# Two query heads per score bank for the first query tile, one bank for the meta scores, and another order of the opening loads

## The reference

```python
h = rms_norm(x, norm_g)
proj = einsum('btd,de->bte', h, w_in)    # q, k, v, gate_a, u_b, gate_b, q_idx, k_idx, w_idx, merge
# 8 heads of 64; one k, one v, one k_idx; rope on q, k, q_idx, k_idx
s = einsum('bqhd,bkd->bqhk', qib, k_idx)                  # the indexer's scores
score = einsum('bqhk,bqh->bqk', relu(s), wib * scale)     # masked by chunk of 64
_, sel = top_k(score, 64)
p = softmax(einsum('bqhd,bqkd->bqhk', qb, k[sel]) * 64 ** -0.5)
attn = einsum('bqhk,bqkd->bqhd', p, v[sel])               # then w_a; a pooling branch, w_b, w_out
```

## Time and profile before

| | |
|---|---|
| median of three runs | 1218.49 us (1218.14 to 1219.87) |
| the profiled execution | 1218.49 us |
| its span, first to last instruction | 1216.7 us |
| PE busy | 1205.7 us (99%), 8521 matmul records |
| PEld busy | 1117.4 us (92%) |
| ACT busy | 726.7 us (60%) |
| DVE busy | 638.6 us (52%) |
| POOL busy | 978.8 us (80%) |
| SP's queue | 207.74 MB, 51.4% of the 16 DMA engines' span |

### The profile page before, as it was taken

How to read it: one execution, slowest core, us unless ns; L and a number is a source line. 1 busy time by engine, 2 the same in 40 slices (tenths; PEclk the granted TensorE clock), 3 DMA queues, 4 the chain that set the end, 5 groups by cost and what they waited for, 6 DMA issues and landing times.

```text
span 1216.7 us, 22059 instructions
## 1 busy us (share of the span) xinstructions
PE 1205.7 (99%) x8521; PEld 1117.4 (92%) x8521; DVE 638.6 (52%) x1463; ACT 726.7 (60%) x1355; POOL 978.8 (80%) x772
## 2 busy tenths in 40 slices
PE   9999999999999999999999999999999999999998
PEld 8999999999998888889999999998889988888886
DVE  6585555765645444312946789853556235444411
ACT  6556756566757666545645677774357347666642
POOL 4775678876679999898889767789899749998795
PEclk9999999999999999999999999999999999999999
DMA  7543445544446555555466645555466435655553
GB/s 254 165 156 122 157 139 184 163 159 137 144 156 199 194 189 188 179 192 189 157 208 211 193 160 176 181 169 190 166 205 226 161 112 178 206 186 183 188 190 104
DMA packets 60056, 213.37 MB, mean 175 GB/s; under 512 B 6672, under 2 KB 6960, under 8 KB 59824
## 3 DMA queue, kind: packets, MB, share of 16 engines
q1 hardware_dynamic: 57600, 207.74, 51.4%
q10 hardware_dynamic: 2352, 4.23, 1.3%
HBM read 210.86 MB, written 1.08 MB: 174 GB/s over the span
## 4 chain that ended last, share of the span: by engine, by line
PE 91%; DVE 6%; ACT 2%; issue 0%; DMA 0%; SPq 0%; DVEq 0%
PE bank L395 23%; PE bank L366 14%; PE bank L368 14%; PE bank L367 14%; PE bank L398 12%; PE bank L1590 2%; PE bank L1592 2%; PE bank L1591 2%; DVE ar L1970 1%; PE bank L1029 1%; PE bank L940 1%; DVE ar L2082 1%; PE bank L2400 1%; PE bank L2402 1%; PE bank L2401 1%; PE bank L2452 1%
## 5 line engine op out<-in xcount | busy, mean ns | idle before, releaser
L325 POOL TENSOR_TENSOR wlo<-raw,whi 128x512 fp32r<-128x512 f32 x768 | 978.6, 1306 | 225.1 <-ACT whi L317 223.8
L317 ACT ACTIVATE whi<-raw 128x1024 fp32r<-128x1024 f32 x387 | 405.0, 1053 | 59.1 <-DMA raw<-w_dram 28.1
L366 PE MATMUL bank<-xx,whi 128*128 128x256 f32 (+1 forms) x1216 | 352.0, 290 | 0.0
L368 PE MATMUL bank<-xx,wlo 128*128 128x256 f32 (+1 forms) x1216 | 343.5, 283 | 0.0
L367 PE MATMUL bank<-xx,whi 128*128 128x256 f32 (+1 forms) x1216 | 343.4, 282 | 0.0
L366 PEld LDWEIGHTS bank<-xx,whi 128*128 128x128 f32 x1216 | 228.8, 188 | 2.8 <-issue 1.2
L367 PEld LDWEIGHTS bank<-xx,whi 128*128 128x128 f32 x1216 | 229.2, 189 | 1.3 <-issue 1.0
L368 PEld LDWEIGHTS bank<-xx,wlo 128*128 128x128 f32 x1216 | 228.6, 188 | 0.0
L395 PE MATMUL bank<-xx,whi 128*128 128x512 f32 x768 | 193.3, 393 | 0.0
L395 PEld LDWEIGHTS bank<-xx,whi 128*128 128x128 f32 x768 | 137.5, 188 | 24.7
L366 PE MATMUL bank<-yy,whi 128*128 128x256 f32 (+1 forms) x390 | 113.3, 291 | 0.0
(11 more groups left out here) (316 smaller groups left out, 1603.8 us busy)
## 6 DMA issues: line engine op xcount, KB each, us to landing
raw<-w_dram SPq DMA_DIRECT2D x387, 512.0 KB, 3.3
ar<-sums_dram ACTq DMA_DIRECT2D x16, 256.0 KB, 4.0
h<-x_dram SPq DMA_DIRECT2D x4, 272.0 KB, 5.9
ar<-mem_dram SPq DMA_DIRECT2D x1, 1024.0 KB, 7.1
out_dram<-ar SPq DMA_DIRECT2D x4, 256.0 KB, 2.2
cst<-con_dram SPq DMA_DIRECT2D x1, 789.0 KB, 7.5
ar<-fin_dram SPq DMA_DIRECT2D x1, 512.0 KB, 5.4
cst<-con_dram SPq DMA_DIRECT2D x1, 134.0 KB, 6.8
```

The source lines that it names most:

```text
L317: e.activation(whi[:, i % NSPL, :], raw[:, i % NRAW, :], ACT.Copy).then_inc(*whi_done.done(i))
L325: return e.tensor_tensor(wlo[:, q, c0:c1], raw[:, i % NRAW, c0:c1], whi[:, q, c0:c1].bitcast(F), ALU.subtract)
L366: e.matmul(o, wh, both[:, 0, :], start=(i == 0), stop=False)
L368: m = e.matmul(o, wl, both[:, 0, :], start=False, stop=(i == len(feed) - 1))
```

## The change

`WARM` goes from 12 to 10. SP loads slot 0 in two halves with the parameters in between, and all pieces of `h` are issued from ACT's queue, at the start of ACT's stream, as five DMAs (chunk 0, chunk 1, then pairs). ACT splits the two halves of slot 0 by themselves; the squares and DVE's additions come behind all high and low parts. `norm_sums` moves from behind the sixth tile of qi 0 to behind the third of qi 1, and `norm_spread` from behind the third tile of qi 1 to behind its eighth and last. ACT splits slot 4 ahead of the norm's root. For query tile 0, in both layers, two heads share a bank, for the indexer's scores (one relu over both) and for the attention's scores (DVE waits for the second of the two); the meta scores lie in one bank.

```diff
--- before.py
+++ after.py
@@ -19,7 +19,7 @@
 TILES = 8
 SLOT = TILES * 128
 NRAW = 4
-WARM = 12
+WARM = 10
 NSPL = 5
 LOOK = 3
 YCOLS = 24 * 256 + 32
@@ -303,6 +303,18 @@
                 e.wait_ge(*low_event(i - NRAW, half))
         e.dma_start(raw[:, i % NRAW, :], None if wts is None else wts[i]).then_inc(sems[f"w{i % NRAW}"], 16)
 
+    def load_half(e, half):
+
+        at = slice(SLOT // 2 * half, SLOT // 2 * (half + 1))
+        e.dma_start(raw[:, 0, at], None if wts is None else wts[0][:, at]).then_inc(sems["w0" if half else "l_w"], 16)
+
+    def split_half(e, half):
+
+        at = slice(SLOT // 2 * half, SLOT // 2 * (half + 1))
+        e.wait_ge(sems["w0" if half else "l_w"], 16)
+        e.activation(whi[:, 0, at], raw[:, 0, at], ACT.Copy).then_inc(*(whi_done.done(0) if half else whi_done.done(0, 0)))
+        split["n"] = half
+
     split = {"n": 0}
 
     def split_high(e, upto):
@@ -337,7 +349,7 @@
 
         slot, j = divmod(len(plan), TILES)
         plan.append(desc)
-        e.wait_ge(*whi_done.of(slot))
+        e.wait_ge(*(whi_done.of(slot) if slot or j >= TILES // 2 else whi_done.of(0, 0)))
         if low:
             low_tile(e, slot, j)
         q = slot % NSPL
@@ -625,30 +637,30 @@
 
     def half_low(e, i, half):
 
-        e.wait_ge(*whi_done.of(i))
+        e.wait_ge(*(whi_done.of(i) if i or half else whi_done.of(0, 0)))
         split_low(e, i, SLOT // 2 * half, SLOT // 2 * (half + 1)).then_inc(*wlo_half.done(i, half))
 
     def prologue_scalar(e):
 
         N, x = norms["n0"], tens["sq"][:, 0, 0:2]
+        for c, n in ((0, 1), (1, 1), (2, 2), (4, 2), (6, 2)):
+            e.dma_start(h[:, c:c + n, :], small[:, c:c + n, :]).then_inc(sems[H_LOADS[c]], 16)
         e.wait_ge(*v_step.of("one"))
         e.activation(x[:, 1:2], x[:, 0:1], ACT.Sqrt).then_inc(*s_step.done("table", "n0"))
-        split_high(e, 1)
+        split_half(e, 0)
         e.wait_ge(sems["l_p"], 16)
         for c in range(8):
             e.wait_ge(sems[H_LOADS[c]], 16)
             norm_high(e, N, c)
-            if c == 1:
-                e.wait_ge(*s_step.of("table", "n0"))
-                norm_square(e, N, 0)
-                norm_square(e, N, 1)
+            if c == 0:
+                split_half(e, 1)
             if c == 3:
-                norm_square(e, N, 2)
                 split_high(e, 2)
         split_high(e, 3)
-        for c in range(3, 8):
+        e.wait_ge(*s_step.of("table", "n0"))
+        for c in range(8):
             norm_square(e, N, c)
-            if c == 4:
+            if c == 2:
                 split_high(e, 4)
         e.wait_ge(sems["l_c1"], 16)
 
@@ -661,10 +673,8 @@
         norm_low(e, N, 0)
         norm_low(e, N, 1)
         half_low(e, 0, 1)
-        norm_add(e, N, 1)
         norm_low(e, N, 2)
         norm_low(e, N, 3)
-        norm_add(e, N, 2)
         half_low(e, 1, 0)
         norm_low(e, N, 4)
         norm_low(e, N, 5)
@@ -672,12 +682,11 @@
         norm_low(e, N, 6)
         norm_low(e, N, 7)
         half_low(e, 2, 0)
-        norm_add(e, N, 3)
-        norm_add(e, N, 4)
+        norm_add(e, N, 1)
+        norm_add(e, N, 2)
         half_low(e, 3, 0)
-        norm_add(e, N, 5)
-        norm_add(e, N, 6)
-        norm_add(e, N, 7)
+        for c in range(3, 8):
+            norm_add(e, N, c)
         e.wait_ge(sems["l_c1"], 16)
 
     def prologue_tensor(e):
@@ -929,12 +938,27 @@
 
     PER_TICK = 2
 
+    def take_scores(e, K, kind, t, hh):
+
+        l = K.l
+        if t:
+            side_.take(e, kind, l, t, hh)
+            side_.give((kind, l, t, hh), (v_step, (kind, l, t, hh)))
+        elif hh % 2 == 0:
+            side_.take(e, kind, l, t, hh // 2)
+            side_.give((kind, l, t, hh // 2), (v_step, (kind, l, t, hh + 1)))
+        return scores_of(K, kind, t, hh)
+
+    def scores_of(K, kind, t, hh):
+
+        nk = K.keys(t)[1]
+        return side_.at(kind, K.l, t, hh)[:, 0:nk] if t else side_.at(kind, K.l, t, hh // 2)[:, nk * (hh % 2):][:, 0:nk]
+
     def indexer_tensor(e, K, t):
         l = K.l
         c0, nk, _ = K.keys(t)
         for hh in range(8):
-            o = side_.take(e, "ix", l, t, hh)[:, 0:nk]
-            side_.give(("ix", l, t, hh), (v_step, ("ix", l, t, hh)))
+            o = take_scores(e, K, "ix", t, hh)
             e.wait_ge(*s_step.of("ki2", l))
             e.wait_ge(*v_step.of("rope", l, "qi", 3))
             e.matmul(o, K.qisc[:, hh, c0:c0 + 128], K.kiT[:, 0:nk], start=True, stop=True).then_inc(
@@ -948,9 +972,13 @@
         l = K.l
         c0, nk, _ = K.keys(t)
         for hh in range(8):
-            o = side_.at("ix", l, t, hh)[:, 0:nk]
             e.wait_ge(*piece.of("ix", l, t, hh))
-            e.activation(o, o, ACT.Relu).then_inc(*s_out.done("ix", l, t, hh))
+            if t:
+                o = scores_of(K, "ix", t, hh)
+                e.activation(o, o, ACT.Relu).then_inc(*s_out.done("ix", l, t, hh))
+            elif hh % 2:
+                o = side_.at("ix", l, t, hh // 2)[:, 0:2 * nk]
+                e.activation(o, o, ACT.Relu).then_inc(*s_out.done("ix", l, t, hh))
             if hh % PER_TICK == PER_TICK - 1:
                 yield
         for _ in range(8 // PER_TICK):
@@ -964,9 +992,9 @@
         for h0 in range(0, 8, PER_TICK):
             yield
             for hh in range(h0, h0 + PER_TICK):
-                e.wait_ge(*s_out.of("ix", l, t, hh))
+                e.wait_ge(*s_out.of("ix", l, t, hh if t else hh | 1))
                 e.wait_ge(*v_step.of("ix", l, t, hh - 1) if hh else v_step.of("w", l))
-                e.scalar_tensor_tensor(ac, side_.at("ix", l, t, hh)[:, 0:nk], K.V[:, t, 64 + hh:65 + hh],
+                e.scalar_tensor_tensor(ac, scores_of(K, "ix", t, hh), K.V[:, t, 64 + hh:65 + hh],
                                        ac if hh else vis, ALU.mult, ALU.add).then_inc(*v_step.done("ix", l, t, hh))
             yield
         for r in range(8):
@@ -1022,8 +1050,7 @@
                 e.wait_ge(*s_step.of("lm", l, t, 7))
                 e.transpose(o[:, 0:128], K.LM, ident).then_inc(*piece.done("pm", l, t))
             for hh in (2 * s, 2 * s + 1) if s < 4 else ():
-                o = side_.take(e, "qk", l, t, hh)[:, 0:nk]
-                side_.give(("qk", l, t, hh), (v_step, ("qk", l, t, hh)))
+                o = take_scores(e, K, "qk", t, hh)
                 e.wait_ge(*v_step.of("rope", l, "q", 3))
                 e.wait_ge(*s_step.of("k2", l))
                 e.matmul(o, K.qcs[:, hh, c0:c0 + 128], K.kT[:, 0:nk], start=True, stop=True).then_inc(
@@ -1082,13 +1109,13 @@
                 e.reciprocal(K.rs[:, hs], K.sm[:, hs]).then_inc(*v_step.done("rs", l, t, s - 2))
             yield
             for hh in (2 * s, 2 * s + 1) if s < 4 else ():
-                e.wait_ge(*piece.of("qk", l, t, hh))
+                e.wait_ge(*piece.of("qk", l, t, hh if t else hh | 1))
                 e.wait_ge(*v_step.of("sel", l, t))
                 if t:
                     e.wait_ge(*s_out.of("pt", l, 0, hh // 2))
                     e.wait_ge(*s_step.of("lm", l, 0, hh))
                 e.wait_ge(*v_step.of("qrec", l))
-                e.scalar_tensor_tensor(K.L[:, hh, 0:nk], side_.at("qk", l, t, hh)[:, 0:nk], K.rq[:, t, hh:hh + 1], bs,
+                e.scalar_tensor_tensor(K.L[:, hh, 0:nk], scores_of(K, "qk", t, hh), K.rq[:, t, hh:hh + 1], bs,
                                        ALU.mult, ALU.add).then_inc(*v_step.done("qk", l, t, hh))
             yield
         ob = side_.at("ob", l, t)
@@ -1114,13 +1141,14 @@
 
     def meta_tensor(e, K):
         l = K.l
-        pair = [side_.take(e, "mqk", l, half) for half in range(2)]
+        o = side_.take(e, "mqk", l)
+        side_.give(("mqk", l), (v_step, ("mqk", l, 1)))
         e.wait_ge(*v_step.of("rope", l, "q", 3))
         e.wait_ge(*s_step.of("k2", l))
         for half in range(2):
-            side_.give(("mqk", l, half), (v_step, ("mqk", l, half)))
             for j in range(4):
-                m = e.matmul(pair[half][0:16, 16 * j:16 * j + 16], K.qcs[:, 2 * j + half, 0:16], K.kT[:, 0:16],
+                at = 64 * half + 16 * j
+                m = e.matmul(o[0:16, at:at + 16], K.qcs[:, 2 * j + half, 0:16], K.kT[:, 0:16],
                              start=True, stop=True)
             m.then_inc(*piece.done("mqk", l, half))
         yield
@@ -1173,9 +1201,9 @@
         rq = K.rq[0:META, 2, :].rearrange("p (j i) -> p i j", i=2)
         e.wait_ge(*v_step.of("mrq", l))
         for half in range(2):
-            e.wait_ge(*piece.of("mqk", l, half))
+            e.wait_ge(*piece.of("mqk", l, 1))
             e.tensor_tensor(Lm[:, 4 * half:4 * half + 4, :],
-                            side_.at("mqk", l, half)[0:META, 0:64].rearrange("p (h k) -> p h k", k=16),
+                            side_.at("mqk", l)[0:META, 64 * half:64 * half + 64].rearrange("p (h k) -> p h k", k=16),
                             rq[:, half, :].unsqueeze(2).broadcast_to([META, 4, 16]), ALU.mult).then_inc(
```

(15 more changed lines are left out.)

## The result

The changed kernel takes 1221.54 us (median of 22 executions, 1218.45 to 1222.51); the kernel before, timed beside it, 1219.02 (22 executions, 1218.08 to 1220.26). The ratio is 1.0017, with a 95% interval of 1.0011 to 1.0023: slower by 0.17%, some 2 us (the medians lie 2.5 us apart). The kernel before spreads over 2.2 us, the changed one over 4.1, in two groups. Seven executions took 1218.45 to 1219.88 (median 1219.16), all at a mean granted clock of TensorE of 0.999. Fifteen took 1220.15 to 1222.51, twelve of them at 0.996 or 0.997 and three at 0.998, which executions of the kernel before show too.

What follows compares the result with a forecast made beforehand. PE, busy 99% of the span, was taken as the bound, so its shifts were added: -0.1 (Part 2) +1.5 (Part 3) -0.8 (Part 4) = +0.6 on 1218.49, giving 1219.1 us; range 1216.8 to 1221.4.

Steps and rivals of the forecast that it cites:

- (a): Rival, opening: two queues land slot 1 by 7.3 us, qi 0 starts 1.7 earlier; 1217.5 us, low end 1217.0; chance 0.18.
- Part 1: Opening: ACT is free at 4.4 us and PE's first matmul starts at 6.2, 1.4 us earlier.
- Part 2: Run up to qi 0: slot 1 lands at 8.8 us, qi 0 starts at 14.1; shift -0.1 us.
- Part 3: Norm's row: a new 1.9 us wait ahead of the keys' squares' sums, the sums' 0.3 wait gone; +1.5 us.
- Part 4: Banks: waits of 0.5 us at the meta scores and 0.4 in layer 1 go; -0.8 us taken.
- (c): Rival, opening turns: TensorE's clock rises later, 48 matmuls each about 0.1 us longer; +3.0 on the sum, 1222.1; chance 0.08.

Runs made afterwards that it cites:

- f1_cover: Changed kernel with 14 warm-up matmuls, four fillers ahead of chunk 1 and eight between the spread and L745; 1218.92 us against 1218.66 for the kernel before.
- e2_opening: Changed kernel without its bank part, so the opening alone; 1222.53 us against 1218.94 for the kernel before.
- e4_sp: Changed kernel with the pieces of h issued from SP's queue again; 1220.77 us against 1218.94 for the kernel before.
- f2_norm_back: Changed kernel with the norm's squares, additions, sums and spread placed as in the kernel before; 1218.29 us against 1218.66 for the kernel before.
- f3_norm_late: Kernel before with the bank part and the later norm, loads and 12 warm-up matmuls as before; 1219.53 us against 1218.66 for the kernel before.
- e1_banks: Kernel before with the bank part of the change alone, opening as before; 1217.18 us against 1218.94 for the kernel before.
- f4_warm10: Kernel before with the bank part and 10 warm-up matmuls in place of 12; 1217.44 us against 1218.66 for the kernel before.
- e3_fill: Changed kernel with 14 warm-up matmuls and four fillers ahead of chunk 1; 1220.39 us against 1218.94 for the kernel before.

## Why the prediction was right and where it was wrong

**The sum at full clock was near, the direction was luck.** The forecast was +0.6. The changed kernel's seven executions at 0.999 have a median of 1219.16, 0.1 over before, and with the fillers of f1_cover the median lies 0.3 over: at full clock the change can't be told from none. The kernel is slower because of the clock's falls, which the forecast left out, and they make 2.3 of the 2.5 us. The measured ratio, +0.17%, is 1220.6 on the predicted base and inside the range; the median, 1221.54, lies 0.1 above its end. Two errors of opposite sign helped: the banks were put 0.4 to 1.0 us too low, and the clock at nothing. The range itself starts at 1216.8, called (a)'s low end, where the working gives 1217.0.

**Part 1.** First matmul at 6.2: it came at 6.78. The price of an issue was right for four of ACT's five (0.41 to 0.45 us, forecast 0.43); the fifth took 0.91. So ACT was free at 4.97, not 4.4. SP's first issues had the same length as before (0.39 to 0.43).

**Part 2.** Slot 1 at 8.8: it landed at 9.0. qi 0 at 14.1: at full clock it started at 13.96 (e2_opening). Of the holes forecast ahead of chunks 1, 2 and 4 only the first appears as idle time there. That the earlier first matmul would be worth little was right: 0.1 was forecast, and the 0.3 measured lies within the 0.5 by which unchanged openings differ. The loads decide, at a share of 1.03 to 1.06 of the DMA engines in the changed kernel. The Trainium skill says in DMA: Bandwidth & Descriptors, "Issuing engines are not separate DMA queues", that issuing from several engines saves only the time of issue. e4_sp agrees with it: SP alone issued slot 1 at 3.53 in place of 2.12, 1.4 us later, and it landed 0.5 us later than in the changed kernel (9.46 against 9.0).

**Part 3.** A new wait of 1.9 us ahead of L745: 1.90, released by ACT's square, as written. Its removal in f2_norm_back and its return in f3_norm_late show that the norm's move alone makes it. Sum of parts 2 and 3: L745 came 1.1 us later at full clock (e2_opening), where -0.1 and +1.5 make +1.4.

**Part 4** had the mechanism right and the size wrong. The term of -0.8 measured -1.8 in the medians of e1_banks and 1.2 to 1.5 in the matched starts. I had read only the idle times of the timeline, 0.45 us ahead of the meta scores and 0.38 in layer 1. They begin where a matmul's modelled end lies, so they hide some idle time: the matched starts of e1_banks moved by 0.5 and 0.55 us at these two places. Two more places had no idle row at all: the last two heads' matmuls of the indexer at 67 to 68 us (0.16 and 0.24 us in the matched starts). That a bank which is free sooner helps there too is my reading; no row shows that wait.

**The step that failed is the price of an idle stretch, and with it the chance of rival (c).** The prediction priced an idle stretch of PE at its own length, and gave the clock 0.08. The clock fell in the profiled execution, and in twelve of 22 the mean clock of 0.996 or 0.997 points to a fall. The size in (c) was near: +3.0 was forecast, and from 8.69 to 14.75 the 27 matmuls lost 0.1 us each, 2.7, and hid some holes; the shift at qi 0 was +2.6. But (c) had the clock rise late, and it had risen: in the changed kernel the warm-up matmuls took 275 ns at 4.8 us, where the kernel before still had 421. It fell again, at 8.1. (c) also lacked the second place. I had called the wait of 1.9 us "a new wait of 1.9 us" and nothing more, though it was longer than any idle time of PE between matmuls in the trace of before (1.2); behind it the fall cost 3.0 us in e2_opening. The deciding point, L426 records of 0.43 us beyond chunk 3, was the right thing to look for.

**What stays open.** What exactly makes the clock fall isn't settled. In the profiled executions f4_warm10's hole of 1.8 us did no harm, e2_opening's and e3_fill's of 1.9 us did, and the same 1.9 us in the changed kernel, e4_sp and f3_norm_late didn't. All that the runs show is that the falls come in some executions, within or just behind such holes, and that with work in both places the eleven executions of f1_cover show no sign of one. The mean clock is a coarse sign. A late rise isn't in it, and 0.998 alone is no proof: the profiled execution of f2_norm_back has 0.998 with no 0.50 in its windows but at the span's end.

## What to carry to other kernels

This PE-bound kernel paid for an idle stretch of PE twice: its length, and in a part of the executions a stretch at half clock behind it, here 2.3 us on the median for the holes of 1.5 and 0.9 us ahead of chunks 0 and 1 and of 1.9 us ahead of L745 (+2.5 against before without fillers, +0.26 with them). So a step that PE waits for must keep work between itself and what feeds it; count the matmuls between the last producer and its first reader before moving either. Take such a change apart before judging it: here one half gained 1.8 us and the other lost 3.6. And match the starts of two traces record by record, since waits shorter than a matmul's latency are in no idle column; but look at more than one execution before trusting half a microsecond of an opening.

## What the runs showed of the hardware

- The column of the granted clock reads 1.00 in the warm-up, while its matmuls took 421 ns and later 275: there only the durations tell. In f2_norm_back the turns began at the lower level, and the clock rose in the middle of them, at about 10.4, while the column reads 1.00 from 9 to 11 us. This execution took 1217.74 us, the second best of its eleven: where PE waits for data anyway, the lower clock cost it little. PE's timeline there:

```profile
9.73 0.43 PE L426 MATMUL bank<-xx,whi 128*128 128x272 f32 x1
9.95 0.43 PE L427 MATMUL bank<-xx,whi 128*128 128x272 f32 x1
...
10.55 0.29 PE L427 MATMUL bank<-xx,whi 128*128 128x272 f32 x1
10.67 0.29 PE L428 MATMUL bank<-xx,wlo 128*128 128x272 f32 x1
```

- The first DMA issues of an engine took 0.39 to 0.45 us each, also when SP and ACT issued at once; later ones took longer. In the kernel before the seventh issue of SP took 0.74 us; in the changed kernel, with both issuing, the fifth of each took 0.71 (SP) and 0.91 (ACT).
- With two issuing queues the rate in 5 to 6 us was 361 to 408 GB/s in the traces of six kernels, with one queue 169 to 280 in six others (273). Still slot 1 landed no earlier for it: at 8.5 to 9.0, where the order of before on one queue gives 8.3 to 8.8. The changed kernel's window, same columns as above:

```profile
5.00:6.00 1.00, 0.32 (x3) 0.13 (x2) 0.38 (x1) 1.00 (x3) 0.00 (x0) 1.00 1.05 361
```
